# Two token tiles of each expert stage computed densely over all experts instead of by gathered rows

## The reference

```python
qr = (hf @ wq).reshape(T, 8, 2, 128)
s = einsum("thpd,hpkd->thpk", qr, keys)           # 128 keys on each of two sides
sv, si = top_k(s, 16)
cand = sv[:, :, 0, :, None] + sv[:, :, 1, None, :]
cid = si[:, :, 0, :, None] * 128 + si[:, :, 1, None, :]
fv, fi = top_k(cand, 16)                          # 8 heads x 16 = 128 picks per token
eid = take_along_axis(cid, fi); gw = softmax(fv)
act = gelu(einsum("tkd,td->tk", u_tab[eid], h))
out = einsum("tk,tkd->td", gw * act, v_tab[eid])  # tables of 128*128 = 16384 experts
```

## Time and profile before

| | us |
|---|---|
| runs: lowest, median, highest | 4409.21, 4415.54, 4416.86 |
| profiled execution: span | 4415.6 |
| PE busy | 3700.6 |
| DVE busy | 3012.2 |
| ACT busy | 1714.2 |
| POOL busy | 1665.2 |
| the two expert stages (first to last matmul of L2770) | 683 to 2336 and 3104 to 4404 |

### The profile page before, as it was taken

One profiled execution on the slowest core, in us unless ns is written; L12 is line 12 of the kernel. 1 busy time (PEld: TensorE's weight loads), 2 busy tenths in 40 slices (PEclk: granted clock), 3 DMA queues, 4 the chain that ended last, 5 costly groups with the idle time before them and its releaser, 6 DMA issues. The chain is left out here.

```text
span 4415.6 us, 55129 instructions
## 1 busy us (share of the span) xinstructions
PE 3700.6 (84%) x18945; PEld 1901.8 (43%) x18945; DVE 3012.2 (68%) x6253; ACT 1714.2 (39%) x5240; POOL 1665.2 (38%) x1510
## 2 busy tenths in 40 slices
PE   7998987988887887887886888888798888888777
PEld 3566843533433433433432335775443343343222
DVE  3964666985875875875875885566797677687444
ACT  2223523444444343444442454352344433433333
POOL 0004503444443444444443432351444344344332
PEclk9999999999999999999998999899999999999999
DMA  8360058999999999999999997004999999999998
GB/s 337 116 252 14 18 186 368 417 421 421 414 421 421 405 421 409 420 419 421 408 416 362 410 394 301 2 18 161 414 419 421 421 413 421 421 410 419 422 421 335
DMA packets 237880, 1513.39 MB, mean 343 GB/s; under 512 B 25536, under 2 KB 30720, under 8 KB 70048
## 3 DMA queue, kind: packets, MB, share of 16 engines
q0 software_dynamic: 184320, 1342.26, 73.7%
q1 hardware_dynamic: 53280, 167.61, 10.1%
HBM read 1497.65 MB, written 12.12 MB: 342 GB/s over the span
## 5 line engine op out<-in xcount | busy, mean ns | idle before, releaser
L2770 PE MATMUL ps<-low,pediag 128*128 128x512 f32 x2304 | 1108.8, 612 | 228.8 <-ACT pediag L2683 227.2
L2545 DVE CUSTOM_DVE_ANT_0 low<-low,hc 128x1024 f32<-128x1024 f32 x576 | 706.1, 1226 | 403.5 <-DMA low<-in_experts_dram,eid 388.0
L2524 POOL DMA_INDIRECT low<-in_experts_dram,eid x570 | 613.5, 1076 | 838.0 <-PE ps L2770 814.7
L2770 PEld LDWEIGHTS ps<-low,pediag 128*128 128x128 f32 x2304 | 405.4, 190 | 860.6 <-ACT pediag L2683 540.4
L2675 ACT ACTIVATE low<-peact 128x1 f32<-128x1 f32 x1152 | 232.2, 202 | 1386.2 <-DVE peact L2545 1385.3
L2770 PE MATMUL ps<-wide,pediag 128*128 128x512 f32 x1280 | 614.6, 614 | 146.3 <-ACT pediag L2683 140.8
L2770 PE MATMUL ps<-wide_last,pediag 128*128 128x512 f32 x1024 | 495.2, 615 | 127.7 <-ACT pediag L2683 123.1
L2524 POOL DMA_INDIRECT wide<-in_experts_dram,eid x316 | 364.1, 1152 | 462.9 <-PE ps L2770 446.8
L2545 DVE CUSTOM_DVE_ANT_0 wide<-wide,hc 128x1024 f32<-128x1024 f32 x320 | 392.3, 1226 | 203.8 <-DMA wide<-in_experts_dram,eid 193.2
L2683 ACT ACTIVATE pediag<-cst,low 128x128 f32<-128x128 f32 x1152 | 462.5, 401 | 37.7
L2545 DVE CUSTOM_DVE_ANT_0 low<-wide_last,hc 128x1024 f32<-128x1024 f32 x256 | 313.8, 1226 | 194.4 <-DMA wide_last<-in_experts_dram,eid 177.9
(11 more groups left out here) (457 smaller groups left out, 4820.5 us busy)
## 6 DMA issues: line engine op xcount, KB each, us to landing
pjdot<-in_mod_t_dram SPq DMA_DIRECT2D x64, 512.0 KB, 5.3
arena<-in_w_mod_dram SPq DMA_DIRECT2D x24, 1024.0 KB, 11.8
arena<-in_peer_wq_dram SPq DMA_DIRECT2D x8, 2048.0 KB, 19.3
qkvT<-x_rows SPq DMA_DIRECT2D x21, 512.0 KB, 8.3
low<-in_experts_dram,eid POOLq DMA_INDIRECT x597, 14.9
pjw<-in_w_cols_dram SPq DMA_DIRECT2D x18, 512.0 KB, 3.7
plw<-in_w_cols_dram SPq DMA_DIRECT2D x18, 512.0 KB, 7.9
wide<-in_experts_dram,eid POOLq DMA_INDIRECT x405, 14.3
```

Source lines behind the costliest of these rows:

```text
L2524: nc.gpsimd.indirect_dma_start(rows[g % RING], None, table, bass.IndirectOffsetOnAxis(eid[:, j % 2, k:k + 1], 0)).then_inc(e_in[g % RING], 16)
L2545: nc.vector.tensor_tensor_reduce(out=dot_out if final else rows[g % RING][:, 0:D], in0=rows[g % RING][:, 0:D], in1=hc[:, j % 2, :], scale= ...
L2770: last = nc.tensor.matmul(ps[:, half, :], diag[:, g % DIAGS, :], rows[g % RING][:, D + half * 512:D + (half + 1) * 512], start=k == 0, sto ...
```

## The change

In each expert stage tiles 1 and 2 no longer gather. For these 256 tokens every one of the 16384 experts is computed. Experts are numbered (i, j) by their two keys. For a fixed second key j there are 128 experts; `dense_dots(j)` multiplies their u rows (a new input table `dense`, laid out so that a plain DMA brings 128 experts of one j) with the 256 tokens' h, eight products of 256 columns into one bank; ACT takes the gelu of the 128x256 result; DVE multiplies it with G, the weights of the picks (zero for experts that a token didn't pick; `weigh`), and `dense_sum(j)` multiplies with the v rows: four products of 512 columns into four banks. That is done for 128 values of j, once for both tiles.

G is built beforehand, four tokens at a time: DVE makes one-hot rows of both key numbers of the 128 picks (`hot_rows`), POOL multiplies one side with the pick weights (`weigh_rows`), PE multiplies the two sides, one 128x128 product a token (`build`), ACT copies to a staging buffer (`take`), and SP spills it to DRAM in 512-byte pieces, to be read back as 128 experts by 256 tokens for four j at a time.

`Plan` lays the stage out in steps. Steps 0 to 127 carry the slots of tile 0; in them the rest of tile 0 and tiles 1, 2 and most of tile 3 are scored, and the 64 batches of G built (steps 60 to 91 and 95 to 126). Steps 128 to 148 carry no slot. From step 149 the slots of the other gathered tiles follow: 3 and 4 in layer 0 (405 steps in all), 3 in layer 1 (277 steps). Dense steps start at step 130, one for each step; in layer 0 from step 150 on one for every second step (the last at 364), in layer 1 still one for each step (the last at 257). The ring of gathered rows shrinks from 8 to 4 buffers during tile 0 and 5 after it. The norm of layer 1's input rows is reordered likewise, and part of the constants is reloaded after the stage, since it lends its space.

```diff
-RING = 8
-AHEAD = 7
+RING = 5
+AHEAD = 4
+DENSE = (1, 2)
+A_RING, GTOK, GBLK, JCH = 4, 4, 32, 4
...
+        self.q = {1: (20, 2), 2: (55, 2), 3: (110, 2), 4: (180, 3), 5: (302, 3)}
+        self.virtual = self.end_of(3) - SLOTS + 2
+        self.slots = list(range(SLOTS)) + [None] * self.virtual + list(range(SLOTS, self.total))
+        self.batch_at = {self.end_of(j) + 3 + b: i * BATCHES + b for i, j in enumerate(DENSE) for b in range(BATCHES)}
+        at = max(self.batch_at) + 4
+        for j in range(NKEYS):
+            self.dense_step.append(at)
+            at += 2 if at > back and ahead else 1
...
+    # SP
+                def load_u(j):
+                    sp.dma_start(u_buf[j % 2], kit.dense[L, j, :, 0:D]).then_inc(u_in[j % 2], 16)
+                def load_v(j):
+                    sp.dma_start(v_buf[j % 3], kit.dense[L, j, :, D:2 * D]).then_inc(v_in[j % 3], 16)
+                    j = plan.dense_at.get(s)
+                    if j is not None and j + 2 < NKEYS:
+                        sp.wait_ge(u_done, j + 1)
+                        load_u(j + 2)
...
+                    j = plan.dense_at.get(s - 2)
+                    if j is not None and j + 3 < NKEYS:
+                        sp.wait_ge(v_done, j + 1)
+                        load_v(j + 3)
...
+    # POOL
+                def weigh_rows(b):
+                    pool.wait_ge(hot_ready, b + 1)
+                    nc.gpsimd.tensor_tensor(hot[b % 2][:, 0], hot[b % 2][:, 0],
+                                            pairs[:, 2, at:at + GTOK][:, :, None].to_broadcast([P, GTOK, P]), ALU.mult
+                                            ).then_inc(hot_weighed, 1)
...
+    # DVE
+                def weigh(j):
+                    dve.wait_ge(act_done, j + 1)
+                    nc.vector.tensor_tensor(out, out, g_buf[j // JCH % 2][:, :, j % JCH, :], ALU.mult).then_inc(coef_ready, 1)
+                def hot_rows(b):
+                    if b >= 2:
+                        dve.wait_ge(built, b - 1)
+                    nc.vector.tensor_tensor(hot[b % 2], iota[:, None, None, :].to_broadcast([P, 2, GTOK, P]), keys, ALU.is_equal
+                                            ).then_inc(hot_ready, 1)
...
+    # ACT
+                def gelu(j):
+                    act.wait_ge(u_done, j + 1)
+                    if j >= 4:
+                        act.wait_ge(v_done, j - 3)
+                    nc.scalar.activation(coef[j % 4], act_bank, ACT.Gelu_apprx_tanh).then_inc(act_done, 1)
...
+    # PE
+                def build(b):
+                    pe.wait_ge(hot_weighed, b + 1)
+                    if b >= 4:
+                        pe.wait_ge(taken, b - 3)
+                    for u in range(GTOK):
+                        last = nc.tensor.matmul(ps[:, 2 + b % 4, u * P:(u + 1) * P], hot[b % 2][:, 0, u, :], hot[b % 2][:, 1, u, :],
+                                                start=True, stop=True)
+                def dense_dots(j):
+                    pe.wait_ge(u_in[j % 2], 16 * (j // 2 + 1))
+                    if j:
+                        pe.wait_ge(act_done, j)
+                    for k in range(KD):
+                        last = nc.tensor.matmul(act_bank, u_buf[j % 2][:, k * P:(k + 1) * P], hT2[:, k, :],
+                                                start=k == 0, stop=k == KD - 1)
+                def dense_sum(j):
+                    pe.wait_ge(v_in[j % 3], 16 * (j // 3 + 1))
+                    pe.wait_ge(coef_ready, j + 1)
+                    for n, i in enumerate(DENSE):
+                        for half in range(2):
+                            last = nc.tensor.matmul(ps[:, dense_bank(i) + half, :], coef[j % 4][:, n * P:(n + 1) * P],
+                                                    v_buf[j % 3][:, half * 512:(half + 1) * 512],
+                                                    start=j == 0, stop=j == NKEYS - 1)
```

More of the change, by code:

```diff
@@ L2404, in peer @@
+def peer(nc, kit, L, tiles, here, qkvT, rows, e_in, room, low, held):
     N, M = len(tiles), here
     DIAGS = 3
-    R_AT = 0
-    F_AT = 2
-    A_AT, A_TURN = 30, 106
+    final = L + 1 == DEPTH
+    ahead = 0 if final else sum(t >= NC for t in tiles[:M])
+    plan = Plan(N, M, ahead)
     LATE = HP - 2 * HEADS_AHEAD
[L2410 to L2413, removed]
@@ L2509, in _ @@
+                store(M - 1)
                 if ahead:
@@ L2527, in _ @@
+                for s in steps:
+                    if s in plan.batch_at:
+                        weigh_rows(plan.batch_at[s])
+                    while issued < plan.total and plan.issued_at(issued) <= s:
+                        gather(issued)
+                        issued += 1
                 if held:
-                    pool.wait_ge(sc.eid_ready, late_numbers + N - 1)
+                    pool.wait_ge(sc.eid_ready, late_numbers + len(plan.summed_tiles))
                     pool.wait_ge(sc.q_ready, HP * (N - 1) + LATE)
@@ new lines, in _ @@
+                for s in steps:
+                    if plan.slots[s] is not None:
+                        dot(plan.slots[s])
+                    if ahead and s == plan.late_at:
+                        dve.wait_ge(n1_in, 48)
+                        nc.vector.scalar_tensor_tensor(out=n1[:, 0, :], in0=n1[:, 0, :], scalar=1.0, in1=n1[:, 2, :],
+                                                       op0=ALU.add, op1=ALU.mult).then_inc(n1_gain, 1)
+                    if s - 1 in plan.dense_at:
+                        weigh(plan.dense_at[s - 1])
+                    if s in plan.batch_at:
+                        hot_rows(plan.batch_at[s])
+                    late_piece(s)
+                    for j in plan.jobs:
+                        piece(j, s)
+                    if s in finish_at:
+                        residual(plan.rank[finish_at[s]])
+                    begun = finish_at if final else next_step
+                    if s - 1 in begun:
+                        mean(plan.rank[begun[s - 1]])
+                    elif s - 2 in begun:
+                        scaled(plan.rank[begun[s - 2]])
@@ new lines, in next_copy @@
+                def next_copy(i, half):
+                    act.wait_ge(turned, plan.turn_no["next", i, half] + 1)
+                    act.wait_ge(n1_gain, 1)
+                    if half == 0 and plan.rank[i]:
+                        act.wait_ge(n1_stored, 16 * plan.rank[i])
+                    for k in range(4 * half, 4 * half + 4):
+                        last = nc.scalar.activation(sc.hT[:, k, :], ps[:, 7, k % 4 * P:(k % 4 + 1) * P], ACT.Identity,
+                                                    bias=n1[:, 1, k:k + 1], scale=n1[:, 0, k:k + 1])
+                    last.then_inc(turn_copied, 1)
@@ L2861, in row_ring @@
         def row_ring(wide):
-            return [wide[:, r * 2 * D:(r + 1) * 2 * D] for r in range(4)] + [low[:, r * 2 * D:(r + 1) * 2 * D] for r in range(4)]
+            return [wide[:, r * 2 * D:(r + 1) * 2 * D] for r in range(4)] + [low[:, 0:2 * D]]
         def mixer_weights(wide):
@@ L2902, in backbone @@
             mix_out(nc, kit, 1, order, o, hT, qkvT, zs, NC, mixer_weights(wide), rows, sems)
-            peer(nc, kit, 1, order, len(order), qkvT, rows, sems, low[:, LOW_Y:LOW], None)
+            peer(nc, kit, 1, order, len(order), qkvT, rows, sems, low[:, LOW_Y:LOW], low[:, 0:LOW_Y], None)
 def constants():
```

768 lines of the change are left out of this document (470 added, 298 removed).

## The result

The changed kernel takes 5079.0 us (median of 4 runs, 5074.6 to 5089.6) against 4416.2 before: 15% slower, ratio 1.1511 with a 95% interval of 1.1494 to 1.1527. The forecast was 5208 us, slower, 5060 to 5430. The profiled execution has a span of 5087.8 us.

The account below looks back on a forecast made before the run. Transfers were taken to bound the kernel, TensorE close behind. Stage A 531, gap 15, dense steps 1392 and 1127, tails 95 and 42 us gave +378 and +414 us on 4415.6: 5208 us, range 5060 to 5430.

Parts of the forecast that it names:

- Transfers bound the kernel before, TensorE close behind: Both expert stages before the change: a slot's 1.05 MB takes 2.49 us at 421 GB/s, its TensorE work 1.72 us.
- Dense steps bound by TensorE: Stage B: TensorE needs 7.05 us a dense step, 902 us a layer; with other work 1392 and 1127 us.
- my lower bound: Dense steps: a half-wide record takes half of 0.429 us, making 6.86 us a step.
- The 2% for waits: Dense steps: 2% added to TensorE's sums, from 1365 to 1392 us in layer 0 and 1105 to 1127 in layer 1.
- The slots of tile 0 bound by VectorE: Steps 0 to 129: VectorE's 477 us plus 27 for GpSimd's disturbance, divided by 0.95, give 531 us a layer.
- the 5%: Slots of tile 0: share put on top of VectorE's work for waits between engines, called the forecast's softest number.
- The gap before the first dense product: Between the stages: last G block written, first u and G loaded, two transfers one after the other; 15 us, 5 to 25.
- Late tables: Dense steps: u loads land as late as gathers, in 14.9 us; 142 us more, 5350 us; chance 0.09.
- GpSimd in a chain that sets the batches: Slots of tile 0: GpSimd's chain makes 64 steps 5.5 us instead of about 4.2; 5374 us; chance 0.14.
- TensorE at its slow rate: Dense steps: same outcome as the forecast but 7.65 us a step, 77 us a layer more, 5362 us; chance 0.12.
- Faster by fewer bytes: Whole kernel: transfers stay the bound, 201 MB less at 421 GB/s saves 478 us, 3938 us; chance 0.02.
- stage A: Steps 0 to 129, the 128 slots of tile 0: forecast 531 us a layer, bounds 482 and about 594.

Follow-up runs that it names:

- half_dots: The changed kernel with dense_dots over four of the eight blocks of 128 columns, every load kept: 4663 us, 416 less.
- light_tables: The changed kernel with all but the first u and v table loads cut to 128 of 1024 columns, same work on every engine: 5081 us, 2 more.

## Why the prediction was right

- **Transfers bound the kernel before, TensorE close behind.** Shown from both sides, by before_less_dma3 (a quarter less of each gather: -427 us) and before_more_pe3 (half as much TensorE work again in a slot: +347 us). But the stretches that I read it from, lie in the first tile of each stage, where a quarter less to move gained next to nothing; there the DMA share of 1.01 misled me, and the reading came out right for the other tiles only.
- **Dense steps bound by TensorE.** Shown: 1336 of 1338 and 1085 of 1087 us busy, half_dots -416 us, light_tables +2 us. The term was 7.05 us a step and measured 6.89. Its mis-sized part is the 256-column record: I took the first projection's busy time over its count, 0.226, which holds tails at each end of a group; the pitch is 0.216, half of the 512-column one, as in my lower bound. That is 21 us a layer. The 2% for waits (27 and 22 us) was not needed either: TensorE sat idle for 2 us in each layer. Together that is 90 of the 94 us by which the dense steps were forecast too long, and these 94 are most of the 120 us between the forecast and the profiled execution (129 to the median). The DMA share there was 0.73 in layer 1, but 0.83 in layer 0, above the 0.6 to 0.75 that I had named.
- **The slots of tile 0 bound by VectorE.** Right as to the engine; that 531 us came so near the measured 529 and 517 (which include the gap) is in part luck. VectorE waited for others for 46 us in layer 0 and 35 in layer 1, where the 5% allowed 27. Its own work is then 483 and 481 us, some 20 of them GpSimd's doing, where I had 504. So one term was too high by over 20 us and the other too low by 19 and 8. Layer 0's part is 13 us longer than layer 1's; VectorE's one wait of 13.6 us for a row of the next norm is of that size, and I had not priced it (I didn't test it apart).
- **The gap before the first dense product.** I had put 15 us; TensorE's wait for the table there is 7.7 us in layer 0 and 7.8 in layer 1.
- **Rivals.** Late tables: out (light_tables). GpSimd in a chain that sets the batches: out, `build` waited for `weigh_rows` for 1.2 and 4.1 us in the two layers; it disturbs, but for 6 us a layer with float32 products and 10 to 12 with float16. TensorE at its slow rate: out, 6.89 us a step against 7.65. Faster by fewer bytes: the bytes went, 203 MB where 201 were computed, and only a version with cheaper products could use them, because it takes TensorE's dense step from 6.89 to 1.73 us, below the 3.95 that the prediction named as the point of no change.
- **Slips in the working.** TensorE's work in the slots of tile 0 is given as some 390 us, its terms add up to 377. The 594 us for the upper end of stage A isn't worked out. Neither bears on the forecast.

The sum was too high in each term but the tails (9 and 5 us longer than forecast) and what lies outside the stages (7 us longer).

## What to carry to other kernels

Before work moves from the bound to an engine that looks free, sum that engine's pitches for both: here a slot's four records of 0.43 us against 24 records of a dense step, and the answer stood in the trace of before. An exchange of transfers for dense products pays only where the products are cheap enough; here a cheaper number format made the difference between 15% slower and 1% faster. When one part of a stage is bound by one engine and the next by another, neither average shows it; read the windows of each part, and don't expect work that is taken from one bound to come back whole: of 95 us taken from VectorE in a layer about 48 came back. A DMA share of 1.0 doesn't say that the transfers are the only bound; a run with fewer bytes does.

## What the runs showed of the hardware that I had not expected

- A float16 product of 128x512 is one record at a pitch near 0.22 us (four in 0.86, 1.03 with the tail), a float32 one two records of 0.43: a quarter of the time. Converting the operands cost 1.05 us on ScalarE for 128x1024 and 0.69 us on VectorE, beside the rest.
- A full DMA share doesn't mean 421 GB/s: plain loads in rows of 4 KB beside gathers in rows of 8 KB moved 387 GB/s at a share of 0.99, and while G was spilled in pieces of 512 bytes the share was 0.83 at 289.
- GpSimd's issue of a gather took 1.07 us on average between 900 and 1190 us of the kernel before, 1.47 in the same stretch of the changed kernel (first row), beside VectorE's one-hot rows and GpSimd's own products, and 1.15 where ScalarE took the products over (second row).

```profile
L2698 POOL DMA_INDIRECT wide<-in_experts_dram,eid x68 | 99.6, 1465 | 66.2 <-PE ps L3004 62.7 <-issue 3.6
```

```profile
L2698 POOL DMA_INDIRECT wide<-in_experts_dram,eid x67 | 77.0, 1150 | 195.2 <-PE ps L3012 192.6 <-issue 2.6
```
